# Two feed-forward first products in one 512-wide matmul per weight block, with VectorE adding the bank's halves

## The reference: what is computed

```python
def squared_relu_mlp(h, w_up, w_down):
    return jnp.square(jax.nn.relu(h @ w_up)) @ w_down        # w_up: 1024 x 4096
```

## Time and profile before

| | |
|---|---|
| median of three runs | 2119.86 us (2115.82 to 2120.2) |
| the profiled execution's own time | 2112.11 us |
| its span, first to last instruction | 2110.3 us |
| TensorE busy | 1901.6 us, 90% of the span |
| VectorE, ScalarE, GpSimd busy | 1130.2, 907.0, 345.0 us |
| mean granted TensorE clock | 0.941 of full speed |

### The profile page before, as it was taken

One profiled execution on the slowest core, in us unless ns is written; L12 is line 12 of the kernel. 1 busy time (PEld: TensorE's weight loads), 2 busy tenths in 40 slices (PEclk: granted clock), 3 DMA queues, 4 the chain that ended last, 5 costly groups with the idle time before them and its releaser, 6 DMA issues.

```text
span 2110.3 us, 29067 instructions
## 1 busy us (share of the span) xinstructions
PE 1901.6 (90%) x12225; PEld 1637.0 (78%) x12225; DVE 1130.2 (54%) x1579; ACT 907.0 (43%) x1396; POOL 345.0 (16%) x396
## 2 busy tenths in 40 slices
PE   5889878999999999968899978898799999999999
PEld 2756657888887888746799868788699978768997
DVE  2455547556574545574455556743455555565554
ACT  3443345344455444633454435432344444434443
POOL 2120222211241212120211120031200005200000
PEclk9899888999999999988999988998999999999999
DMA  8454453454656666320656533310245554504553
GB/s 275 140 202 140 160 179 124 157 170 158 204 171 202 216 226 210 126 80 11 209 180 189 181 100 111 115 54 1 96 159 180 189 170 173 176 1 140 180 184 135
DMA packets 217966, 320.61 MB, mean 152 GB/s; under 512 B 8550, under 2 KB 123946, under 8 KB 217452
## 3 DMA queue, kind: packets, MB, share of 16 engines
q1 hardware_dynamic: 212628, 308.96, 44.8%
q0 software_dynamic: 1744, 6.03, 0.8%
q10 hardware_dynamic: 3464, 3.75, 0.5%
HBM read 317.68 MB, written 1.05 MB: 151 GB/s over the span
## 4 chain that ended last, share of the span: by engine, by line
PE 74%; DVE 12%; ACT 6%; DMA 4%; POOL 2%; issue 2%; SPq 0%; POOLq 0%; ACTq 0%; DVEq 0%
PE ps L69 71%; DVE WLO L86 3%; PE ps L77 3%; DVE AR L96 2%; ACT WHI L80 1%; DVE AR L86 1%; DMA RAW<-in_w_mod_dram 1%; DMA RAW<-in_w_up_dram 1%; DMA RAW<-in_w_in_dram 1%; ACT AR L80 1%; POOL SM L86 1%; DVE SM L99 1%; ACT XR L80 1%; ACT L80 1%; POOL XR L86 1%
## 5 line engine op out<-in xcount | busy, mean ns | idle before, releaser
L86 DVE TENSOR_TENSOR WLO<-RAW,WHI 128x1024 fp32r<-128x1024 f32 (+2 forms) x506 | 593.8, 1215 | 426.8 <-ACT WHI L80 426.6
L80 ACT ACTIVATE WHI<-RAW 128x1024 fp32r<-128x1024 f32 (+2 forms) x506 | 488.2, 1014 | 396.0 <-PE ps L69 287.1
L69 PE MATMUL ps<-TH,WHI 128*128 128x256 f32 x1672 | 485.0, 290 | 27.1 <-DVE WLO L86 15.8
L69 PE MATMUL ps<-TL,WHI 128*128 128x256 f32 x1672 | 479.5, 287 | 0.0
L69 PE MATMUL ps<-TH,WLO 128*128 128x256 f32 x1672 | 479.3, 287 | 0.0
L69 PE MATMUL ps<-WHI,ARR 128*128 128x512 f32 x1120 | 355.6, 394 | 5.6 <-DVE ARR L86 3.1
L69 PEld LDWEIGHTS ps<-TH,WHI 128*128 128x128 f32 x1672 | 327.3, 196 | 38.5 <-issue 24.7
L69 PEld LDWEIGHTS ps<-TL,WHI 128*128 128x128 f32 x1672 | 327.3, 196 | 0.3
L69 PEld LDWEIGHTS ps<-TH,WLO 128*128 128x128 f32 x1672 | 326.7, 195 | 0.2
L69 PE MATMUL ps<-WHI,TH 128*128 128x512 f32 (+2 forms) x608 | 240.3, 395 | 24.1 <-DVE WLO L86 22.8
L69 PEld LDWEIGHTS ps<-WHI,ARR 128*128 128x128 f32 x1120 | 211.0, 188 | 56.8 <-issue 9.3
(11 more groups left out here) (187 smaller groups left out, 1947.7 us busy)
## 6 DMA issues: line engine op xcount, KB each, us to landing
RAW<-in_w_mod_dram SPq DMA_DIRECT2D x48, 1024.0 KB, 5.4
RAW<-in_w_up_dram SPq DMA_DIRECT2D x48, 1024.0 KB, 5.4
RAW<-in_w_down_dram SPq DMA_DIRECT2D x48, 1024.0 KB, 5.2
RAW<-in_ffn_w_in_dram SPq DMA_DIRECT2D x44, 1024.0 KB, 5.1
RAW<-in_w_in_dram SPq DMA_DIRECT2D x20, 1024.0 KB, 5.3
RAW<-in_ffn_w_out_dram SPq DMA_DIRECT2D x20, 1024.0 KB, 5.0
RAW<-in_dil_w_in_dram SPq DMA_DIRECT2D x18, 1024.0 KB, 4.8
RAW<-in_gdn_w_in_dram SPq DMA_DIRECT2D x16, 1024.0 KB, 5.8
```

The lines of the kernel that those rows point to most:

```text
L69: return Made(None if self.eng is None else self.eng.matmul(o, l, r, start=start, stop=stop))
L80: return Made(None if self.eng is None else self.eng.activation(o, i, f, **k))
L86: return Made(None if self.eng is None else self.eng.tensor_tensor(o, a, b, op))
```

## The change

For the first products of all feed-forwards, TH and TL become the two halves of one tensor TT. For each (f, k) pair one matmul of 512 columns takes the high weights against [TH | TL] and writes the whole bank; one of 256 columns takes the low weights against TH and adds to the bank's first half. So each half f of a tile has a bank of its own, and the product is the sum of the bank's two halves. VectorE makes this sum with a reduction over a view of the bank (`dve_halves`), one for each half tile, and that frees the bank. ScalarE's Relu and Silu then read the sum from SBUF. In the gated feed-forwards the product gate times up moves from VectorE to GpSimd (`pool_ffn`), and the rounding and subtraction behind it stand one tile pair later.

```diff
         def pe_cols_half(key, t, f, nt, cs, need):
+            fs = slice(128 * f, 128 * f + 128)
+            x2 = T2v(nt)
+            banks.take((key, f), gring)
+            wait_free((key, f))
+            b = banks.of((key, f))
+            both, first = b.rearrange("p (s t) -> p s t", s=2), b[:, 0:256]
             for k in range(8):
                 pe.wait_ge(dve_w, ("lo", t.i, k // 4))
                 need(k)
-                m = pe.matmul3(o, hi[:, k, 128 * f:128 * f + 128], lo[:, k, 128 * f:128 * f + 128], xh[:, k, cs], xl[:, k, cs], k == 0, k == 7)
-            return m
+                if k > 0:
+                    pe.matmul(first, lo[:, k, fs], x2[:, 0, k, cs], False, False)
+                m = pe.matmul(both, hi[:, k, fs], x2[:, :, k, cs], k == 0, k == 7)
+                if k == 0:
+                    pe.matmul(first, lo[:, k, fs], x2[:, 0, k, cs], False, False)
+            m.then_inc(pe_gemm, ("acc", key, f), *([("used", t.i)] if f == 1 else []))

+        def dve_halves(signal, o, key, f, *said):
+            b = banks.of((key, f))
+            dve.wait_ge(pe_gemm, ("acc", key, f))
+            dve.reduce(o, b.rearrange("p (s t) -> p t s", s=2), ALU.add).then_inc(signal, ("free", (key, f)), *said)

         def act_up(l, sq, hc, c):
-            act.wait_ge(pe_gemm, ("acc", bank))
-            wait_tmp(act, l, sq, key)
-            act.act(t, banks.of(bank), ACT.Relu).then_inc(act_hd, ("free", bank), ("relu", key))
+            act.wait_ge(dve_hd, ("sum", key, 1))
+            act.act(t, t, ACT.Relu).then_inc(act_hd, ("relu", key))

         def dve_work(l, sq):
             for s in range(len(WORK[l]) + AFTER):
                 w, _ = step_of(l, s)
+                v, done = step_of(l, s - 1)
+                if v[0] == "up":
+                    dve_upsum(l, sq, *v[1:])

+        def pool_ffn(l):
+            for c in range(11):
+                ta, tb, _, _ = ffn_parts(c)
+                pool.wait_ge(act_hd, ("fs", l, c))
+                pool.wait_ge(dve_hd, ("sum", l, c, 1, 1))
+                pool.tt(tb, ta, tb, ALU.mult).then_inc(pool_hd, ("fm", l, c))

         def dve_ffn(l, t):
+            def rest(c):
+                _, tb, hi, lo = ffn_parts(c)
+                dve.wait_ge(act_hd, ("fh", l, c))
+                dve.tt(lo, tb, hi.bitcast(F32), ALU.subtract).then_inc(dve_hd, ("f", l, c))
             for c in range(11):
-                dve.tt(tb, ta, banks.of((("fu", l, c), 0)), ALU.mult).then_inc(dve_hd, ("free", (("fu", l, c), 0)), ("fm", l, c))
+                for x, o in enumerate(ffn_parts(c)[0:2]):
+                    dve_splits(tile_of["ffn_w_in_2", l, 0, FFH * x + 256 * c])
+                    if c >= 1 and x == 0:
+                        rest(c - 1)
+                    if c >= 4:
+                        dve.wait_ge(*((pool_hd, ("fm", l, c - 4)) if x == 0 else (dve_hd, ("f", l, c - 4))))
+                    for f in range(2):
+                        dve_halves(dve_hd, o[:, 256 * f:256 * f + 256], ("f", l, c, x), f, ("sum", l, c, x, f))
```

More of the change, by code:

```diff
@@ L1834, in need @@
                     pe.wait_ge(dve_tn, ("lo", f"mlp{l}", ti, k // 4))
-            key = ("up", l, sq, hc, c)
             t = use("w_up", (l, sq), 0, 8, 128 * per(l) * hc + 256 * c, 256)
[L1837 to L1842, removed]
+            pe_cols_half(("up", l, sq, hc, c), t, f, 512, slice(256 * sq, 256 * sq + 256), need)
         def up_tile(l, sq, hc, c):
@@ L1849, in up_parts, with dve_upsum @@
             return ("u", l, sq, hc, c), *[x[:, 2 * c:2 * c + 2, :].rearrange("p f t -> p (f t)") for x in hidden(l, sq)]
+        def dve_upsum(l, sq, hc, c, f):
+            key, _, _ = up_parts(l, sq, hc, c)
+            wait_tmp(dve, l, sq, key)
+            dve_halves(dve_hd, tmp(l, sq, key)[:, 256 * f:256 * f + 256], ("up", l, sq, hc, c), f, ("sum", key, f))
         def act_up(l, sq, hc, c):
             key, hi, _ = up_parts(l, sq, hc, c)
[L1853 removed]
             t = tmp(l, sq, key)
[L1855 to L1857 removed]
+            act.wait_ge(dve_hd, ("sum", key, 1))
+            act.act(t, t, ACT.Relu).then_inc(act_hd, ("relu", key))
             act.wait_ge(act_hd, ("relu", key))
@@ L2835, in pe_ffn @@
             for c in range(11):
-                pe_cols(("fg", l, c), "ffn_w_in_2", l, 256 * c, need)
-                pe_cols(("fu", l, c), "ffn_w_in_2", l, FFH + 256 * c, need)
+                for x in range(2):
+                    w = use("ffn_w_in_2", l, 0, 8, FFH * x + 256 * c, 256)
+                    for f in range(2):
+                        pe_cols_half(("f", l, c, x), w, f, 256, slice(0, 256), need)
             def lhs(k, ti):
@@ L2845, in pe_ffn, with ffn_parts, rounded @@
             pe_out(("fd", l), fd_spec(l), lhs, hid, t)
+        def ffn_parts(c):
+            return FTM[2 * c % 8], FTM[(2 * c + 1) % 8], *[v[:, 2 * c:2 * c + 2, :].rearrange("p f t -> p (f t)") for v in (FHH, FHL)]
         def act_ffn(l, t):
+            def rounded(c):
+                _, tb, hi, _ = ffn_parts(c)
+                act.wait_ge(pool_hd, ("fm", l, c))
+                act.act(hi, tb, ACT.Copy).then_inc(act_hd, ("fh", l, c))
             for c in range(11):
+                ta = ffn_parts(c)[0]
@@ L2849, in act_ffn @@
                 act_splits(tile_of["ffn_w_in_2", l, 0, 256 * c])
-                ta, tb = FTM[2 * c % 8], FTM[(2 * c + 1) % 8]
-                act.wait_ge(pe_gemm, ("acc", ("fg", l, c), 0))
-                if c >= 4:
-                    act.wait_ge(dve_hd, ("fm", l, c - 4))
-                act.act(ta, banks.of((("fg", l, c), 0)), ACT.Silu).then_inc(act_hd, ("free", (("fg", l, c), 0)), ("fs", l, c))
+                if c >= 1:
+                    rounded(c - 1)
+                act.wait_ge(dve_hd, ("sum", l, c, 0, 1))
```

38 lines of the change are left out of this document (20 added, 18 removed).

## The result

The changed kernel takes 2109.3 us (median of six runs, 2103.66 to 2112.45), the kernel before 2118.9, measured beside it (2115.82 to 2120.57). The ratio is 0.9953, with a 95% interval from 0.9937 to 0.9968: 9.6 us by the medians, 6.8 to 13.3 by the interval. The forecast was 2106.0 and a gain of 13.9 us. The profiled execution took 2109.12 us, its span 2107.3, and the mean granted clock was 0.941, as before.

The account below looks back on a forecast made before the run. TensorE's matmul stream was taken to bound the first products. The gain was 19.0 - 2.4 (latent waits) - 1.7 (saving only waited for) - 1.0 (context) = 13.9 us, so the median 2119.9 becomes 2106.0, range 2094 to 2117.

Parts of the forecast that it names:

- What bounds the kernel: Stretches of first products last as long as TensorE's matmul stream, so its savings count in full while VectorE keeps up.
- so I take 0.0133: First products: each (f, k) pair saves one matmul's fixed part, 0.0133 us; 19.6 us over 1472 pairs, 19.0 after clock shares.
- The sum: VectorE's 184 half-tile sums take 0.69 us each, 127 us in all, hidden in gated feed-forwards up to 1.0 us a sum.
- Cost nothing: Layer 1's MLP: the sums fit into VectorE's waits, 4.4 of 5.55 us, and banks come free in time, so no cost.
- 1 us for what it delays (0 to 5): Context's MLP: VectorE gets 5.5 us more work in each such stretch, and the delays cost 1 us, range 0 to 5.
- a sign of being wrong: The prediction is wrong if, among other signs, waits for VectorE appear in the context's MLP.
- the 14 of the forecast: Latent tokens' MLP of layer 0: TensorE's waits on WLO and ARR grow from 10.1 to some 14 us.
- 5.1 us (2.4 + 3.4 - 0.7): Forecast by stage: context's MLP 2.4 us saved, layer 1's MLP 3.4 saved, latent tokens' MLP 0.7 lost.
- crowding takes back what the MLPs gain: Rival: VectorE's crowding in the MLPs takes their gain, leaving 4 to 9 us, so 2111 to 2116; chance 0.15.

Follow-up runs that it names:

- one piece: Changed kernel with the high and low part of each token block side by side in the gated feed-forwards, so 512 moving columns are one piece: 0.9950 of before.
- transpose repeated: Changed kernel with one transpose of the first norm issued 33 times instead of once, which moves later instruction packets: 2108.6 us, 0.9958 of before.
- sum behind: Changed kernel with each half's sum in the MLPs moved behind the splits of its step instead of ahead of them: 1.0126 of before.
- grouped: Changed kernel with each half tile's eight 512-wide matmuls together and its eight 256-wide ones behind them: 0.9966 of before.
- layer 0, context as before: Two kernels, the changed one with both layer 0 MLPs as before (0.9959 of before), or only the context's MLP as before (0.9946, 2105.7 us).

## Why the prediction came out as it did

*What bounds the kernel.* Right: with the feed-forwards alone changed, time follows TensorE's stream, and 44 of 92 tiles give nearly all of the gain.

*The fixed part of a matmul.* Right in kind, too large in size. The step "so I take 0.0133" measured 10.3 ns a pair: 1472 pairs give 15.2 us, not 19.6, and each feed-forward 3.6 us instead of 4.7 (128.4 to 124.8, not 123.7). By the columns at one per cycle, the wide one has a fixed part of 17 (in a row) to 20 ns (beside narrow ones), where the second products had 13.3. The Trainium skill, "TensorE: Matmul & The Clock Gate", section "Back-to-back issue gap", gives an isolated matmul 2.5 ns beyond its columns, so by that estimate 2.5 ns a pair would be saved; the trace of this stream shows 10.3, and disagrees with it as the rows of before did.

*The sum.* Right: 0.685 us, 184 times, hidden in the gated feed-forwards. The room was smaller than the forecast's (0.8 us a sum rather than 1.0), since the price of GpSimd's neighbourhood was counted against the spare time but not in VectorE's loop. That price itself was right: the Trainium skill, "SBUF — State Buffer", section "Who interferes with whom", agrees with 3.20 and 3.45 us against 2.36.

*Layer 1's MLP.* "Cost nothing" was nearly right: 1.6 us gained of the 2.6 that 256 pairs can give. The second of its two stretches of first products shortens by 1.4 us in every trace, as much as 128 pairs can give; the first gives less, 0.5 in the first traces, and its windows show a granted clock of 0.95 in place of 0.97.

*Layer 0.* The step that failed is "1 us for what it delays (0 to 5)" in the context's MLP. With 256 pairs it should have gained 2.6 us, and it lost 2.5, so the delay cost 5.1 us (6.5 in the second profile), at and over the upper end. It is also what the prediction named as a sign of being wrong: waits of TensorE for VectorE's WLO (0.93 us) and ARR (1.19 us) appear in the context's MLP, where the trace of before has neither. The second products account for 2.6 us of it; about 1.1 us (an estimate) is the clock's, since the stretch of first products behind them runs 5.0 us at the lower clock in place of 2.9. The row that spoke against a low value was among those read: the windows over first products show VectorE busy for 20.85 of 33 us, but the loss came in the second products between them, where VectorE was busy for 23.34 of 27.00, and that window wasn't read. TensorE busy for 29.00 of 29 us says that there is no wait yet, not how near one is. In the latent tokens' MLP the waits grew from 10.1 to 12.9 us, near to the 14 of the forecast, but a part of that hangs on where an instruction packet falls, which the sum knew nothing of.

*The sum of it.* With measured sizes: 7.0 (feed-forwards) + 1.6 (layer 1) - 2.5 (context) leaves 6.1 us, and the latent stage is 1.9 us longer by the means of its two traces each; the whole measured 6.8 to 13.3. The stages' bill is thus below the interval's low end. The rest lies outside the changed MLPs, and it goes with the granted clock. From the end of the first feed-forward's first products to the end of the second's, with how long the granted clock was the lower one (1.2 GHz) in it:

| | stretch, us | at the lower clock, us |
|---|---|---|
| before, both traces | 382.5, 382.5 | 27.3, 27.3 |
| MLPs alone changed | 378.0 | 17.1 |
| changed kernel, first and second trace | 375.5, 378.0 | 17.1, 23.9 |
| two others with the feed-forwards changed (one piece; transpose repeated) | 375.5, 375.5 | 17.1, 17.1 |
| five others (feed-forwards alone; sum behind; grouped; layer 0, context as before) | 378.0 each | 23.9 each |

The second feed-forward's own gain is 3.6 us of this. The other 0.9 to 3.4 us go with the clock, and the row of the MLPs alone shows the clock's part by itself: 4.5 us less, with nothing in the stretch changed and 10.2 us less at the lower clock. Why the clock is low for longer in one execution than in another of the same program is open.

So the total came out better than the mechanism. The forecast gave the MLPs 5.1 us (2.4 + 3.4 - 0.7), and with the MLPs alone changed the kernel gained nothing (1.0008). Of the rivals, "crowding takes back what the MLPs gain" (2111 to 2116) describes what happened; the total, 2109.3, lies between it and the forecast, and that it lies within the stated range is in part luck.

## What to carry to other kernels

Merging matmuls saves only the fixed part of each one that goes, some 10 ns here, whatever the durations of single matmuls suggest; it pays where the engine that does the extra work has room in every stretch it serves, so read that engine's windows over the stretches between the changed ones too. Work that stands in the chain to the next product and frees a bank goes ahead of work that has slack: the same 96 sums a few instructions later cost 36 us more, about half of it in waits and up to half by the lower clock that went with them. A gain of a few us in a program this long has to be shown by stages and medians, since a stage with nothing changed in it can move by as much, through the granted clock alone; so read the time at the lower clock beside each stage.

## What the runs showed of the hardware

- 512-wide matmuls with weights stationary and tokens moving follow each other every 230 ns (233.7 beside narrow ones), with tokens stationary every 226.7. Neither the two pieces of the operand nor the alternation is the cause.
- Reductions of 128x512 from PSUM to 256 outputs, with the two addends 256 elements apart, take 0.68 us each and start 0.60 us apart in a row: outputs cost nothing.
- A 16384-byte instruction packet that starts in the middle of a 1 MB load goes with a last piece 1.4 to 1.7 us behind the other fifteen, in six traces of six, and in three others it was elsewhere or at the load's very start and no piece was late. Moving it gave the stretch 2.9 us back, and the total nothing that could be measured.
- The time at the lower clock differs between two executions of one program: 17.1 and 23.9 us of one and the same stretch, which took 375.5 and 378.0 us.
